# A state-space stage in a two-block network kernel: decay rows stored by chunk, weight tiles asked for one place earlier, and a fifth output half-tile ahead of the group's norm

## The reference, cut to what matters

```
def ssd_chunked_scan(xs, dt, A, Bm, Cm):        # 8 chunks of L = 128 tokens, 4 groups of 8 heads
    def step(state, inp):
        acum = cumsum(dt_k * Ag, axis=1)
        decay = exp(where(causal, acum[:, :, None] - acum[:, None, :], -inf))
        cb = einsum('blgn,bsgn->blsg', C_k, B_k)
        y_intra = einsum('blsgh,bsghp->blghp', cb[..., None] * decay, x_k * dt_k[..., None])
        y_inter = einsum('blgn,bghpn->blghp', C_k, state) * exp(acum)[..., None]
        ...
def mamba2_mixer(...):
    ...                                          # z, x, B, C from u @ w_in; conv and silu on x, B, C
    y = ssd_chunked_scan(...) + d_skip * xs
    y = y.reshape(bsz, s, D_INNER) * silu(z)
    y = rms(y.reshape(bsz, s, N_GROUPS, D_INNER // N_GROUPS)) * y_g   # one norm per group
    return y @ w_out
```

## Time and profile before

| what | value |
|---|---|
| three runs | 3521.37 us median, 3518.78 to 3530.22 |
| the profiled execution, its own time | 3521.37 us |
| its span, first to last instruction | 3519.9 us |
| PE busy | 3181.3 us (90% of the span) |
| DVE, ACT, POOL busy | 53%, 39%, 21% of the span |
| mean granted TensorE clock | 0.946 |
| the four groups of `stage_ssm` | about 1484 to 2405 us |

### The profile page before, as it was taken

How to read it: one execution, slowest core, us unless ns; L and a number is a source line. 1 busy time by engine, 2 the same in 40 slices (tenths; PEclk the granted TensorE clock), 3 DMA queues, 4 the chain that set the end, 5 groups by cost and what they waited for, 6 DMA issues and landing times. The chain is left out here.

```text
span 3519.9 us, 41749 instructions
## 1 busy us (share of the span) xinstructions
PE 3181.3 (90%) x15532; PEld 2634.1 (75%) x15532; DVE 1852.6 (53%) x2499; ACT 1359.8 (39%) x1876; POOL 725.3 (21%) x488
## 2 busy tenths in 40 slices
PE   7999999999997999588988989988889999998799
PEld 5788878888885777476766857767768888887677
DVE  4344215666665322556556555576346776766433
ACT  4333114555554312333222222233236666666331
POOL 2110002222221001202021030120224444443110
PEclk8999999999999999699999989999989999998899
DMA  2111221211211212012121131121111111111211
GB/s 93 44 49 44 77 78 54 61 55 55 67 55 42 102 66 96 21 42 66 42 52 51 42 73 35 48 56 60 61 54 37 37 37 37 37 41 44 108 66 60
DMA packets 83049, 197.35 MB, mean 56 GB/s; under 512 B 6304, under 2 KB 41760, under 8 KB 82624
## 3 DMA queue, kind: packets, MB, share of 16 engines
q1 hardware_dynamic: 74048, 164.66, 15.2%
q0 software_dynamic: 8832, 30.41, 2.8%
HBM read 165.56 MB, written 21.10 MB: 53 GB/s over the span
## 5 line engine op out<-in xcount | busy, mean ns | idle before, releaser
L114 ACT ACTIVATE whi<-wraw 128x1024 fp32r<-128x1024 f32 x208 | 218.4, 1051 | 501.0 <-PE ssm_pT L127 142.7
L119 DVE TENSOR_TENSOR wlo<-wraw,whi 128x1024 fp32r<-128x1024 f32 x176 | 252.0, 1432 | 237.1 <-ACT whi L114 233.8
L125 PE MATMUL ssm_D<-x1hi,whi 128*128 128x512 f32 x640 | 263.0, 411 | 4.4 <-DVEq L1725 4.4
L125 PE MATMUL b_D<-x1hi,whi 128*128 128x512 f32 x640 | 255.0, 398 | 8.0 <-DVEq L999 6.6
L126 PE MATMUL ssm_D<-x1lo,whi 128*128 128x512 f32 x640 | 254.8, 398 | 0.0
L127 PE MATMUL ssm_D<-x1hi,wlo 128*128 128x512 f32 x640 | 254.7, 398 | 0.0
L126 PE MATMUL b_D<-x1lo,whi 128*128 128x512 f32 x640 | 250.7, 392 | 0.0
L127 PE MATMUL b_D<-x1hi,wlo 128*128 128x512 f32 x640 | 250.6, 392 | 0.0
L2156 DVE TENSOR_TENSOR_SCAN stick_keep<-stick_keep 128x896 f32<-128x896 f32 (+7 forms) x128 | 210.6, 1650 | 37.4 <-ACT stick_keep L2071 36.2
L125 PE MATMUL stick_D<-x1hi,whi 128*128 128x512 f32 x512 | 213.7, 417 | 7.4 <-DVE x1lo L152 7.4
L2299 POOL TENSOR_TENSOR stick_rows<-stick_rows,stick_keep 128x896 f32<-128x896 f32 (+7 forms) x128 | 156.9, 1228 | 296.0 <-DVE stick_keep L2156 293.6
(11 more groups left out here) (385 smaller groups left out, 8099.7 us busy)
## 6 DMA issues: line engine op xcount, KB each, us to landing
wraw<-w_dram SPq DMA_DIRECT2D x208, 512.0 KB, 3.5
sq<-acum_rows SPq DMA_DIRECT2D x32, 512.0 KB, 8.7
att_bias<-alibi_dram SPq DMA_DIRECT2D x16, 512.0 KB, 3.5
stack<-stack POOLq DMA_DIRECT2D x32, 256.0 KB, 3.6
x_sb<-xT_dram SPq DMA_DIRECT2D x8, 512.0 KB, 8.0
branch_a<-sq POOLq DMA_DIRECT2D x8, 512.0 KB, 3.5
y_b<-att_y POOLq DMA_DIRECT2D x8, 512.0 KB, 3.0
f<-y_b SPq DMA_DIRECT2D x2, 2048.0 KB, 8.8
```

The costliest lines, as they stand in the source:

```text
L114: act.activation(self.whi[:, s, :, :], self.wraw[:, s, :, :], ACT.Copy).then_inc(self.w_hi, 1)
L119: dve.tensor_tensor(self.wlo[:, s, :, :], self.wraw[:, s, :, :], self.whi[:, s, :, :].bitcast(F32), ALU.subtract).then_inc(self.w_lo, 1)
L125: pe.matmul(out, self.whi[:, s, w0, :], xhi[:, k, cols], start=start, stop=False)
```

## The change

Three things are done, all in the Mamba-2 mixer:

1. `acum_dram` is laid out as chunk, head, token. A chunk's eight rows are then one run of 4 KB instead of eight runs of 512 B that lie 4 KB apart. `stage_dt` writes the table with pieces of 512 B.
2. On SP, seven weight loads instead of six stand ahead of the first row, and each later load stands two rows earlier.
3. In the output product, half-tile 4 goes to the bank `pS`, and PE makes it before the norm's sums. The other half-tiles are spread over five banks by a table, so that each waits for the last half-tile of its own bank.

```
-                sp.dma_start(acum_dram, rows[:, :]).then_inc(stored, 16)
+                sp.dma_start(acum_dram.rearrange("c h t -> h c t"),
+                             rows[:, :].rearrange("h (c t) -> h c t", c=NC)).then_inc(stored, 16)
...
-        banks = [D[:, 0:H], D[:, H:S], pX[:, :], pT[:, :]]
+        spaces = [D[:, 0:H], D[:, H:S], pX[:, :], pT[:, :], pS[:, :]]
+        BANK_OF = (0, 1, 2, 3, 4, 2, 3, 0, 1, 2, 3, 0, 1, 2, 3, 4)
+        banks = [spaces[b] for b in BANK_OF]
+        LAST_USE = [max([e for e in range(o) if BANK_OF[e] == BANK_OF[o]], default=None) for o in range(2 * KT)]
...
-                        sp.dma_start(E[c % 2], acum_dram[bass.ds(8 * g, GH), c * P:c * P + P]
+                        sp.dma_start(E[c % 2], acum_dram[c, bass.ds(8 * g, GH), :]
                                      .partition_broadcast(P)).then_inc(row_land[c % 2], 16)
 
-                    for m in range(6):
+                    for m in range(7):
                         load(m)
                     for c in range(NC):
                         row(c)
                         if c % 2 == 1:
-                            load(6 + c // 2)
-                    for m in range(10, 14):
+                            load(7 + c // 2)
+                    for m in range(11, 14):
                         load(m)
...
                     for o in range(4):
                         out_products(o, GT - 1).then_inc(dn, 1)
+                    pe.wait_ge(K.w_lo, GROUP_TILES * g + (n0 + 12))
+                    pe.wait_ge(st_done, 9 * g + 9)
+                    for k in range(GT):
+                        last = out_products(4, k)
+                    last.then_inc(dn, 1)
                     pe.wait_ge(acc_done, 3 * g + 3)
                     K.norm_sums(pe, pCB, sums_done)
                     K.norm_spread(pe, pY, rtok_done, g + 1, spread_done)
-                    for o in range(4, 2 * KT):
+                    for o in range(5, 2 * KT):
                         if o % 4 == 0:
                             pe.wait_ge(K.w_lo, GROUP_TILES * g + (n0 + 11 + o // 4))
-                        pe.wait_ge(evac, OUTS * g + (20 + o - 1))
+                        pe.wait_ge(evac, OUTS * g + (20 + LAST_USE[o] + 3))
...
-        acum_dram = nc.dram_tensor("acum_rows", (SH, S), F32, kind="Internal").ap()
+        acum_dram = nc.dram_tensor("acum_rows", (NC, SH, P), F32, kind="Internal").ap()
```

More of the change, by code:

```diff
@@ L1476, in out_products @@
                         j, half = o // 2, o % 2
-                        return K.products(pe, banks[o % 4], j // 2 % 2, 4 * (j % 2) + k, k, yhi, ylo, half,
+                        return K.products(pe, banks[o], j // 2 % 2, 4 * (j % 2) + k, k, yhi, ylo, half,
                                           k == 0, k == GT - 1)
@@ L1716, in group @@
                             dve.wait_ge(dn, OUTS * g + (20 + 2 * j + half + 1))
-                            dve.tensor_tensor(tmp[:, cols], banks[(2 * j + half) % 4], Rg[:, cols],
+                            dve.tensor_tensor(tmp[:, cols], banks[2 * j + half], Rg[:, cols],
                                               ALU.mult).then_inc(evac, 1)
```

## The result

| | before | after |
|---|---|---|
| median of the runs beside each other | 3522.03 us (3518.78 to 3530.22) | 3486.53 us (3480.44 to 3492.72) |
| ratio, 95% interval | | 0.9896, 0.9870 to 0.9921 |
| profiled execution: span | 3519.9 us | 3482.3 us |
| the four groups, us each | 229.6, 228.7, 232.1, 234.2 | 222.4, 218.4, 221.8, 224.2 |

The kernel is 35.5 us faster at the median and 37.6 us in the profiled executions. The forecast was 54.4 us faster. The time of 3486.5 lies inside the range (3452 to 3490), but above the likeliest case's own (3457 to 3478). It lies nearest to the 3489 us that were worked out for rows that stay slow, and the rows did not stay slow.

A forecast was written before the change was run, and what follows sets the result against it. PE, busy for 90% of the span, was taken as the bound. Terms of -35.0 (first wait), -30.8 (scan), +0.3 (table write) and +11.1 (half-tile) sum to -54.4 us, from 3521.4 to 3467 us; range 3452 to 3490.

The forecast's parts named there:

- likeliest case: Whole kernel: all terms hold, 3467 us with its own range of 3457 to 3478; chance 0.76.
- rows that stay slow: Row fetch: rival in which a row still needs 8 us, time 3489 us (halfway 3479); chance 0.13 with both sizes.
- The first wait: PE's first turn-in of each group (L1429): earlier load of weight tile 8 removes all four waits, -35.0 us.
- The sign named: New trace: the 8 to 9 us wait at each group's first L1429 is gone, and ACT's wait for `wraw` too.
- The rows' transfer: Fetch of a chunk's row: median falls from 8.7 us to 3.5 to 4.5 us, number of pieces being the limit.
- the slower one: Row fetch: rival in which rows come later than today; 12 us rows would give 3542 us; chance 0.04.
- The scan's pace: Turn-in of chunk 1 to products of chunk 7: 7.7 us less a group, -30.8 us in four.
- Without lateness it would be made of: Same stretch: 1.47, 7.19, five times the steady 8.01 and 9.76 us, sum 58.5 against a mean of 66.2.
- L1442's 7.9 us vanish: PE's waits for the weighed decay, 7.9 us in total, disappear.
- L1450's 20.1 fall to 10 or so: PE's waits at the turn-outs fall from 20.1 us to about 10.
- comes from the order of slots: Chunk 6 to 7: PE's own wait of 1.8 us for `y_sb` comes from slot order and stays.
- The half-tile: Half-tile 4 ahead of the norm: PE's stop behind the spread grows by 2.78 us a group, +11.1 us in four.

The follow-up runs named there:

- e5: The changed kernel with one more wait: POOL takes a chunk's row only when DVE has weighed the chunk before; 3470.86 us, ratio 0.9849.
- e2: The kernel before with only the rows laid out by chunk, old load queue and old norm; 3468.98 us, ratio 0.9842.
- e1: The kernel before with only the weight loads asked for earlier, old table and old norm; 3481.97 us against 3523.80, ratio 0.9875.
- e9: The changed kernel with e5's wait, e7's half-tile placement and bank table, and DVE's low split of tiles 9 and 10 one slot later; 3426.28 us, ratio 0.9724.
- e3: The kernel before with only half-tile 4 ahead of the norm's sums and the five banks; 3534.76 us, ratio 1.0031.
- e6: The changed kernel with another bank table, half-tile 5 going to the bank that is emptied first; 3466.84 us, ratio 0.9841.
- e7: The changed kernel with e6's bank table and half-tile 4 moved from ahead of the norm's sums to behind its spread; 3456.92 us, ratio 0.9824.

## Why the prediction was right and where it failed

**The range: right, and in part by luck.** Its upper end of 3490 stands there for rows that stay slow. The rows were quick, and what brought the time up to 3486.5 was something that the forecast didn't have.

**The first wait: right in size, half right in cause.** 33.4 of 35.0 us. What is missing is less than the 2.7 us that e5 gains in this piece, where the low split of tile 8 no longer stands behind POOL. The sign named (ACT's wait for `wraw` gone) held. But e2 shows that quick rows alone give it too, and e1 that the loads alone do. With both in the sum, one of them gives almost nothing more.

**The rows' transfer: right in size, its reason unproven.** 3.5 to 4.5 us were chosen between bounds of 3.5 and 8.7; it is 3.7. The rival of rows that stay slow is out, and so is the slower one. The reading that half-idle DMA engines point to the number of pieces doesn't carry much. In the kernel before, while two slow rows moved and a weight load stood behind them, the engines read as fully busy and brought 71 GB/s:

```profile
1566.00:1568.00 2.00, 2.00 (x11) 1.61 (x10) 0.01 (x1) 1.06 (x1) 0.00 (x0) 1.00 1.07 71
```

And while one quick row moves, their share over the whole transfer is 0.52, no more than it was, at 175 GB/s; in its best stretch it is 0.90 at 344:

```profile
1578.50:1581.50 3.00, 3.00 (x18) 2.46 (x17) 2.59 (x5) 0.38 (x1) 0.00 (x0) 1.00 0.52 175
1579.00:1580.00 1.00, 1.00 (x7) 0.78 (x6) 1.00 (x2) 0.00 (x0) 0.00 (x0) 1.00 0.90 344
```

So a slow row took about twice the busy time of a quick one, not only idle time (0.45 of 7 us against 0.52 of 3). Which of the three things that the layout changes makes the row quick, the number of pieces, their size or that they lie in one run, no run here separates.

The Trainium skill (page "DMA: Bandwidth & Descriptors", section "Why small descriptors are slow") gives a packet about 3 cycles beyond its 32-byte beats, 19 against 16 for 512 B and 131 against 128 for 4 KB. From that I had an estimate of 7.5 us for the row in one run. It does not describe this transfer, which fell from 8.7 to 3.7 us.

**The scan's pace: this step failed.** "Without lateness it would be made of" steady slots, sum 58.5 us; it is 62.5. I took every slot that the row made long to be whole again. Two things stood behind the row, and the working had neither:

- POOL's work moved in time with the row, from idle moments of DVE into DVE's weighing. The forecast asked what a quick row brings to POOL, and not beside whom POOL then runs. e5 puts this at 9.4 of the 16.4 missing us, and at 2.7 more in the first piece.
- The slot from 2 to 3 had a second late thing of almost the same length, the silu and split ahead of DVE's skip term. It was hidden, since DVE waited for the row anyway, and the turn-out waits of 20.1 us were its sign. In e5 the two pieces from turn-in to chunk 7 sum to 60.1 against 58.5, so it is worth about 6.6 us in four groups. With the 9.4 that makes 16.0 of 16.4. By an estimate from e5's rows 2.5 of the 6.6 are POOL again: the low split in this slot takes 1.86 instead of 1.23 us behind POOL's mask, 0.63 us in each group. The slot follows the split: in the changed kernel the split there takes 1.48 us and the slot 9.44, both 0.38 less than in e5.

The forecast's "L1442's 7.9 us vanish" and "L1450's 20.1 fall to 10 or so" were wrong for these two reasons in turn (7.7 and 16.7). The wait of 1.8 us at chunk 7 did stay, but not because it "comes from the order of slots": e9 changes no slot of PE, and the longest such wait falls to 1.3. A group takes 218.4 to 224.2 us, not 216 to 219.

**The half-tile: right, to the hundredth in the stop.** 4.98 instead of 2.20 us, 2.78 more in each group, as the rows of DVE said. e3 alone cost 11.0 us, forecast 11.1, and e6 takes it back with the table alone. I had added nothing for the longer time at half clock. It is there, but small: behind the stop of 2.2 us eleven or twelve matmuls start further than 0.23 us apart and lose 2.3 us at the mean, behind 5.0 us it is thirteen or fourteen and 2.9 us, about 2.2 us more in four groups. It didn't show in the sum (9.8), since another piece became shorter, in the main because the clock fell less there. Windows over the piece from chunk 7 to the sums, one a group, after the change:

```profile
1635.03:1668.04 33.01, 29.93 (x125) 23.17 (x126) 22.26 (x36) 13.61 (x15) 0.00 (x0) 0.90 0.06 17
1855.65:1886.75 31.10, 26.79 (x124) 21.27 (x125) 22.27 (x36) 13.61 (x15) 0.00 (x0) 1.00 0.05 17
2072.96:2108.38 35.42, 31.11 (x124) 24.24 (x125) 22.27 (x36) 13.61 (x15) 0.00 (x0) 0.87 0.05 15
```

(the length in us stands first behind the stretch, and behind the busy times come the granted clock, the DMA share and GB/s). At a granted clock of 1.00 the piece takes 31.10 us with the half-tile. Without it, in e7, it takes

```profile
1636.91:1665.31 28.40, 24.10 (x112) 19.02 (x113) 22.26 (x36) 13.62 (x15) 0.00 (x0) 1.00 0.06 19
```

28.40 us. The difference of 2.7 us is just the twelve matmuls, so the half-tile filled no hole. What the four groups after took on top of 31.1 us was 6.6 us, all at a granted clock below 1.00. Those before took 10.1 us on top of 28.4 (29.58, 30.46, 33.21 and 30.43), but 1.2 of it in a group whose granted clock was 1.00:

```profile
1645.99:1675.57 29.58, 24.32 (x113) 18.94 (x114) 22.41 (x36) 14.67 (x16) 1.27 (x2) 1.00 0.06 19
```

There PE idled about 1 us longer, 0.8 of it before the weighed decay of chunk 7. So of the 3.5 us that the change seemed to gain in this piece, 2.3 go with the clock and 1.2 don't.

## What to carry to other kernels

When a late transfer stops being late, redraw the queues of the engines around it, at their new times. Look for the next late thing in the same slot, and for two engines that now work at once and did not before. A pair of DVE and POOL on data in SBUF is such a pair, and a wait of the one that has time (POOL here) can be worth more than the transfer's last microsecond. A wait that keeps two engines apart can push them together somewhere else, as in e5, so their other work is looked at too. Gains of two cures for one wait are tested each alone before they are added. And filler work pays where the engine stands still: the same half-tile cost 11 us ahead of the norm, nothing with another table, and behind the spread it took the whole stop away.

## What the runs showed of the hardware

- **DVE and POOL exclude each other** on tiles in SBUF, and 0.02 to 0.16 us decide who pays. A DVE product of two SBUF tiles of 128x1024 takes 1.22 us alone and 2.90 to 2.95 behind a POOL subtraction. That subtraction takes 1.90 alone and 2.82 behind DVE, a POOL mask 1.09 alone and 1.80. DVE's low split of a weight tile takes 1.23 alone, 1.86 behind a mask and 2.96 behind a subtraction.
- **The layout of the source sets a transfer's time.** For the same 512 KB, 1024 pieces of 512 B took 8.7 us and 128 of 4 KB 3.7. If it is the number of pieces, that is about 5.6 ns for each further one, an estimate from these two times. That all 128 partitions read the same 4 KB cost 0.2 us at most (3.7 against 3.5 for a weight tile).
- **A load behind slow rows is issued slowly too.** SP took 4.20 us to issue the weight load behind two rows of 1024 pieces, and 0.33 behind two rows of 128.
- **The granted clock falls in some groups and not in others of one execution**, with the same work on PE: 33.01, 31.10 and 35.42 us in the rows above. A piece that long without its clock beside it can't be compared to a microsecond, and a single profiled run may stand several us from its kernel's median (e6: a span of 3475.7 at a median of 3466.8; e7: 3448.0 at 3456.9). What makes it fall in one group and not the next stays open.
